# A second feed-forward product by seven products of quarters in place of eight, in network one

## Chip, core and metric

One core of one Trainium2 chip runs the whole program: two networks of two layers each, one after the other. Engines are named TensorE (PE), VectorE (DVE), ScalarE (ACT), GpSimd (POOL) and SyncE (SP). The metric is the device time of one execution in microseconds; the kernel before takes 3363.85 us (median of three).

## What is computed

Of the reference, the part that the change touches is the end of each layer of network one, at `SEQ` = 512 tokens, `D_MODEL` = 1024, `D_FF` = 4096, in float32:

```python
x = x + jnp.concatenate([o_a, o_b, o_c], axis=-1) @ w_out[l]
hf = rmsnorm(x, g_mlp[l])
x = x + jnp.square(jax.nn.relu(hf @ w_ff1[l])) @ w_ff2[l]
```

The second product, (512 x 4096) times (4096 x 1024), is what is computed in another way. Network two and the rest of network one stay as they are.

## The kernel before

Every float32 product is made of three products of `fp32r` halves (`product`, line 262): high by high, high by low, low by high. So each weight tile of 128 rows and 512 columns is split first: ScalarE rounds it to its high half (`make_hi`, line 233, or 235 where a gain is multiplied in) and VectorE subtracts that from the tile for the low half (`make_lo`, lines 245 and 248). Both halves go to `whl`, which holds two chunks of four tiles; chunk j may be split when TensorE is through with chunk j - 2 (`chunk_used`). The chunks come from HBM over SyncE into a ring of four slots of 1 MB (`load_up_to`); a slot is loaded again when its last chunk's low halves are made.

The stage is `out_and_feed_forward` (line 1754). After the output projection and the norm, the 4096 hidden features are taken in two halves of 2048. For each half:

- `ReluSquared`: the first product, for four feature tiles (128 features x 512 tokens) at a time, in four PSUM banks, over two weight chunks (eight depth tiles). ScalarE takes the relu of a bank (line 1729), VectorE multiplies it with the bank (line 1745) into `y`, ScalarE makes its high half (line 1710) and VectorE its low half (line 1714) in `u`.
- `ResidualAdd`: the second product, with `u` as the stationary operand and the weights moving, for two halves of 512 output columns, four chunks of weights each, four token tiles per chunk. VectorE adds each finished bank to `x` (line 685).

What each engine does, and in which order, is written out by hand in the methods `tensor`, `scalar`, `vector` and `gpsimd` of these classes. In this stage GpSimd only raises four values to a power (line 702). A second product of one half has 16 depth tiles x 4 token tiles x 2 column halves x 3 = 384 matmuls, so that 2048 features cost 384 and 1024 cost 192.

```python
(sh, sl), (mh, ml) = stationary, moving
nc.tensor.matmul(bank, sh, mh, start=start, stop=False)
nc.tensor.matmul(bank, sh, ml, start=False, stop=False)
return nc.tensor.matmul(bank, sl, mh, start=False, stop=stop)
```

The same classes of work also occur elsewhere and are read from there: line 1944 is a GpSimd product of 512 columns in network two, lines 876 to 883 are rotations on GpSimd in the first stage, and line 1897 is a VectorE step that reads PSUM.

Of the kernel before, what the change touches and what calls it, by code (L numbers as in the profile page):

```python
# [8 lines left out]
F32 = mybir.dt.float32  # L9
# [6 lines left out]
P = 128  # L16
# [65 lines left out]
def chunks_of(rows, cols, width=512, deep=4, row0=0, col0=0):  # L82
# [7 lines left out]
A_HALF, B_HALF = D_FF // 2, D_FF2 // 2  # L90
# [4 lines left out]
    ("w_ff1", chunks_of(DM, A_HALF)), ("w_ff2", chunks_of(A_HALF, DM)),  # L95
    ("w_ff1", chunks_of(DM, A_HALF, col0=A_HALF)), ("w_ff2", chunks_of(A_HALF, DM, row0=A_HALF // P)),
]
B_WEIGHTS = [
# [29 lines left out]
class Core:  # L128
# [38 lines left out]
    def start_layer(self, weights, drams, prefix, l):  # L167
        self.queue, self.offsets, at = [], [], {}
        for name, chunks in weights:
            for k, kt, n, w in chunks:  # L170
# [34 lines left out]
class SplitWeights:  # L205
# [52 lines left out]
    def wait_tile(self, pe, j, k):  # L258
        pe.wait_ge(self.lo_made, self.tiles[j] + k + 1)

# [1418 lines left out]
class ReluSquared:  # L1679

    def __init__(self, c, w, j0, i, F, hl, u, r, y, sems, free):
        self.c, self.w, self.j0, self.base, self.F, self.hl = c, w, j0, i * F, F, hl
        self.u, self.r, self.y, self.free, self.n_group = u, r, y, free, i * F // 4
        self.filled, self.relu_done, self.squared, self.his, self.los = sems

    def tensor(self, pe):
        w, c, hl = self.w, self.c, self.hl
        for g in range(self.F // 4):  # L1690
            for j in (self.j0 + 2 * g, self.j0 + 2 * g + 1):
                row, kt = w.plan[j][0:2]
                for b in range(4):
                    if row == 0:
                        self.free(pe, g, b)
                    for k in range(kt):
# [3 lines left out]
                        ins = product(c.nc, c.banks((4 * g + b) % 8), (w.part(j, 0, k)[:, s], w.part(j, 1, k)[:, s]),  # L1700
# [7 lines left out]
    def high(self, act, f):  # L1708
        act.wait_ge(self.squared, self.base + f + 1)
        self.c.nc.scalar.copy(self.u[:, 0, f, :], self.y[:, f % 4, :]).then_inc(self.his, 1)  # L1710

    def low(self, dve, f):
        dve.wait_ge(self.his, self.base + f + 1)
        self.c.nc.vector.tensor_tensor(self.u[:, 1, f, :], self.y[:, f % 4, :], self.u[:, 0, f, :].bitcast(F32),
                                       ALU.subtract).then_inc(self.los, 1)

    def scalar(self, act):
        for g in range(self.F // 4):
            j = self.j0 + 2 * g
            self.w.make_hi(act, j + 2)  # L1720
            for b in range(4):
                f = 4 * g + b
                if b == 3:
                    act.wait_ge(self.c.chunk_used, self.w.first + j + 2)
                else:
                    act.wait_ge(self.filled, 3 * (self.n_group + g) + b + 1)
                if self.base + f >= 4:
                    act.wait_ge(self.squared, self.base + f - 3)
                self.c.nc.scalar.activation(self.r[:, f % 4, :], self.c.banks(f % 8), ACT.Relu
                                            ).then_inc(self.relu_done, 1)  # L1730
                if f:
                    self.high(act, f - 1)
            self.w.make_hi(act, j + 3)
        self.high(act, self.F - 1)

    def vector(self, dve):
        for g in range(self.F // 4):
            j = self.j0 + 2 * g
            self.w.make_lo(dve, j + 2)
            for b in range(4):  # L1740
                f = 4 * g + b
                dve.wait_ge(self.relu_done, self.base + f + 1)
                if self.base + f >= 4:
                    dve.wait_ge(self.los, self.base + f - 3)
                self.c.nc.vector.tensor_tensor(self.y[:, f % 4, :], self.c.banks(f % 8), self.r[:, f % 4, :],
                                               ALU.mult).then_inc(self.squared, 1)
                if f >= 2:
                    self.low(dve, f - 2)
            self.w.make_lo(dve, j + 3)
        self.low(dve, self.F - 2)  # L1750
        self.low(dve, self.F - 1)


def out_and_feed_forward(c, mix, hl, gain, half, u, r, y):
# [3 lines left out]
    F = A_HALF // P  # L1758
    with ExitStack() as ctx:
        sb = lambda n, s: ctx.enter_context(nc.sbuf_tensor("aff_" + n, s, F32))  # L1760
        ssq, rstd, junk = sb("ssq", [P, TT, 2]), sb("rstd", [P, TT, 1]), sb("junk", [P, BANK])
        xn = y[:].rearrange("p f s -> p (f s)").rearrange("p (b n) -> p b n", b=2)
        with c.stage("aff", "hi", "lo", "mix_turned", "mix_his", "mix_los", "out_filled", "out_added", "squares",
                     "meaned", "rooted", "rows", "x_turned", "x_his", "x_los", "up_filled", "relu_done", "squared",
                     "u_his", "u_los", "down0_filled", "down0_added", "down1_filled", "down1_added", "end_squares") as (
                block, hi_made, lo_made, mix_turned, mix_his, mix_los, out_filled, out_added, squares,
                meaned, rooted, rows, x_turned, x_his, x_los, up_filled, relu_done, squared,
                u_his, u_los, down0_filled, down0_added, down1_filled, down1_added, end_squares):
            ups, downs = (4, 20), (12, 28)
            gains = {j: gain for j0 in ups for j in range(j0, j0 + 8)}  # L1770
            w = SplitWeights(c, ctx, "aff_", 36, hi_made, lo_made, gains)
# [8 lines left out]
                               (ssq, rstd, junk[:], xn, half))  # L1780

            def up_free(i):
                def free(pe, g, b):
                    if g >= 2:
                        pe.wait_ge(squared, i * F + 4 * (g - 1))
                    elif i == 0:
                        pe.wait_ge(x_los, 8)
                    else:
                        pe.wait_ge(down0_added, TT * (g + 1))
                return free  # L1790
            up = [ReluSquared(c, w, ups[i], i, F, hl, u, r, y, (up_filled, relu_done, squared, u_his, u_los),
                              up_free(i)) for i in range(2)]
            down = [ResidualAdd(c, w, pair(downs[i], 4), of(u), i * F, x, None,
                                ((down0_filled, down1_filled)[i], (down0_added, down1_added)[i]) + (None,) * 4,
                                lambda pe, n, t, i=i: pe.wait_ge(squared, i * F + F - 4 * (1 - n)),
                                lambda pe, n, t, k, i=i: pe.wait_ge(u_los, i * F + k + 1) if n == t == 0 else None)
                    for i in range(2)]
# [6 lines left out]
            def _(pe):  # L1804
# [3 lines left out]
                for i in range(2):  # L1808
                    up[i].tensor(pe)
                    down[i].tensor(pe)  # L1810
                pe.wait_ge(down1_added, 1)
                c.stay_busy(pe, 0, 40)

            @block.scalar
            def _(act):
# [5 lines left out]
                for i in range(2):  # L1821
                    up[i].scalar(act)
                    down[i].scalar(act)
                for t in range(TT):
                    act.wait_ge(down1_added, TT + t + 1)
# [5 lines left out]
            @block.gpsimd  # L1831
            def _(pool):
                out.gpsimd(pool)

            @block.vector
            def _(dve):
# [5 lines left out]
                for i in range(2):  # L1842
                    up[i].vector(dve)
                    down[i].vector(dve)
# [1660 lines left out]
def first_block(c, d, cst, layers=DEPTH):  # L3505
# [11 lines left out]
    with nc.Fori(0, layers) as l, ExitStack() as ctx:  # L3517
# [87 lines left out]
        with ExitStack() as right:  # L3605
            hl = split_tile(right)
            with nc.sbuf_tensor("a_shift", [P, 24], F32), \
                    nc.sbuf_tensor("a_u", [P, 2, A_HALF // P, SEQ], F32R) as u, \
# [268 lines left out]
```

## Time and profile before

| | |
|---|---|
| runs | 3363.85, 3378.34, 3363.09 us; median 3363.85 |
| profiled execution | span 3368.7 us from the first to the last instruction |
| granted TensorE clock, mean | 0.980 |
| TensorE busy | 3198.9 us, 95% |
| VectorE busy | 1884.3 us, 56% |
| ScalarE busy | 1311.1 us, 39% |
| GpSimd busy | 394.5 us, 12% |

The profiled execution's own time is told by its span alone; it lies 4.9 us above the median of the runs. Busy times of TensorE count each matmul from its start to its modelled end, so they overlap; the pace of matmuls is read from one start to the next. A line L245 is a line of the kernel before; where a helper issues an instruction the line is the helper's. The stage of the change lies at 308 to 721 us in layer 1 and at 1022 to 1435 us in layer 2.

### The profile page before, as it was taken

To read this page: it belongs to the slowest core of one execution; us is meant where nothing else is said; L and a number is where in the kernel's file an instruction comes from. 1 tells how busy PE (TensorE), PEld (TensorE's weight loads), DVE (VectorE), ACT (ScalarE), POOL (GpSimd) and SP (SyncE) were. 2 spreads that over 40 slices of the span, in tenths; PEclk is the share of its full clock that TensorE was granted. 3 is DMA by queue.
4 is the path that set the end of the run, shared out by engine and by line. 5 is a ranking of instruction groups with operands and counts; after the bars stand their busy time and mean duration, and the time that the engine had idled before them with its cause. 6 is when DMAs were issued, how large, how long until landed. Compare 5 with 4: busy or idle time off the path is not lost. (4 is left out here: it accounts for less than half of the span.)

```text
span 3368.7 us, 49442 instructions
## 1 busy us (share of the span) xinstructions
PE 3198.9 (95%) x19200; PEld 2657.4 (79%) x19200; DVE 1884.3 (56%) x3610; ACT 1311.1 (39%) x2780; POOL 394.5 (12%) x368
## 2 busy tenths in 40 slices
PE   8998999999989999979999999999899989999996
PEld 6877888877777888868867888888788768888885
DVE  4875443336865434247486457474475865574644
ACT  4455433334354424134363333233443543332324
POOL 1021000000030000003013302010012034010100
PEclk9999999999999999989899999999999999999998
DMA  4111222222102222132100122222222000222221
GB/s 166 54 51 38 88 100 88 88 77 86 66 1 76 100 97 91 38 123 94 51 1 2 40 71 100 97 99 85 81 97 74 1 1 5 91 94 102 91 99 42
DMA packets 37345, 239.58 MB, mean 71 GB/s; under 512 B 4464, under 2 KB 5232, under 8 KB 15088
## 3 DMA queue, kind: packets, MB, share of 16 engines
q1 hardware_dynamic: 36528, 234.21, 19.5%
q8 instruction: 158, 2.59, 0.3%
q10 hardware_dynamic: 576, 2.10, 0.2%
q14 instruction: 83, 0.68, 0.1%
HBM read 234.19 MB, written 2.10 MB: 70 GB/s over the span
## 5 line engine op out<-in xcount | busy, mean ns | idle before, releaser
L265 PE MATMUL ps<-b_hl,bff_whl 128*128 128x512 f32 x704 | 274.1, 389 | 3.1 <-DVE b_hl L630 3.1
L267 PE MATMUL ps<-b_hl,bff_whl 128*128 128x512 f32 x704 | 273.9, 389 | 0.0
L266 PE MATMUL ps<-b_hl,bff_whl 128*128 128x512 f32 x704 | 273.9, 389 | 0.0
L248 DVE SCALAR_TENSOR_TENSOR bff_whl<-ring,b_cols,bff_whl 128x512 fp32r<-128x512 f32 (+1 forms) x224 | 153.2, 745 | 197.3 <-ACT bff_whl L235 197.0
L245 DVE TENSOR_TENSOR aff_whl<-ring,aff_whl 128x512 fp32r<-128x512 f32 x160 | 99.8, 686 | 223.1 <-ACT aff_whl L233 223.1
L235 ACT ACTIVATE bff_whl<-ring,b_cols 128x512 fp32r<-128x512 f32 (+1 forms) x224 | 136.6, 682 | 176.4 <-PE ps L267 176.4
L266 PE MATMUL ps<-aff_whl,a_u 128*128 128x512 f32 x512 | 204.3, 399 | 0.0
L265 PE MATMUL ps<-a_hl,aff_whl 128*128 128x512 f32 x512 | 199.4, 390 | 3.1 <-DVE a_hl L630 3.1
L265 PE MATMUL ps<-aff_whl,a_u 128*128 128x512 f32 x512 | 201.7, 394 | 0.0
L267 PE MATMUL ps<-aff_whl,a_u 128*128 128x512 f32 x512 | 200.7, 392 | 0.0
L266 PE MATMUL ps<-a_hl,aff_whl 128*128 128x512 f32 x512 | 199.2, 389 | 0.0
L267 PE MATMUL ps<-a_hl,aff_whl 128*128 128x512 f32 x512 | 199.2, 389 | 0.0
L265 PE MATMUL ps<-ain_whl,a_hl 128*128 128x512 f32 (+3 forms) x512 | 189.3, 370 | 9.4 <-issue 6.2
L233 ACT CAST aff_whl<-ring 128x512 fp32r<-128x512 f32 x160 | 87.5, 621 | 275.9 <-PE ps L267 271.3
L266 PE MATMUL ps<-ain_whl,a_hl 128*128 128x512 f32 (+3 forms) x512 | 186.2, 364 | 0.0
L267 PE MATMUL ps<-ain_whl,a_hl 128*128 128x512 f32 (+3 forms) x512 | 186.0, 363 | 0.0
L245 DVE TENSOR_TENSOR bff_whl<-ring,bff_whl 128x512 fp32r<-128x512 f32 x128 | 84.6, 720 | 144.2 <-ACT bff_whl L233 144.2
L265 PEld LDWEIGHTS ps<-b_hl,bff_whl 128*128 128x128 f32 x704 | 132.1, 188 | 30.9 <-DVE b_hl L630 3.6
L248 DVE SCALAR_TENSOR_TENSOR aff_whl<-ring,a_gains,aff_whl 128x512 fp32r<-128x512 f32 x128 | 87.6, 746 | 122.3 <-ACT aff_whl L235 122.1
L267 PEld LDWEIGHTS ps<-b_hl,bff_whl 128*128 128x128 f32 x704 | 132.2, 188 | 27.6
L266 PEld LDWEIGHTS ps<-b_hl,bff_whl 128*128 128x128 f32 x704 | 132.2, 188 | 27.3
L233 ACT CAST bff_whl<-ring 128x512 fp32r<-128x512 f32 x128 | 70.4, 621 | 210.3 <-PE ps L267 202.8
(510 smaller groups left out, 7826.8 us busy)
## 6 DMA issues: line engine op xcount, KB each, us to landing
ring<-in_a_w_ff SPq DMA_DIRECT2D x64, 1024.0 KB, 4.6
ring<-in_b_w_up SPq DMA_DIRECT2D x32, 1024.0 KB, 4.8
ring<-in_a_w_in SPq DMA_DIRECT2D x16, 1024.0 KB, 4.9
ring<-in_b_w_down SPq DMA_DIRECT2D x16, 1024.0 KB, 4.6
ring<-in_b_w_in_att SPq DMA_DIRECT2D x12, 1024.0 KB, 4.6
ring<-in_b_w_up SPq DMA_DIRECT2D x16, 768.0 KB, 4.1
ring<-in_b_w_in_conv SPq DMA_DIRECT2D x12, 768.0 KB, 4.2
ring<-in_a_w_out SPq DMA_DIRECT2D x8, 1024.0 KB, 4.7
```

The costliest lines, as they stand in the source:

```text
L233: self.c.nc.scalar.copy(self.part(j, 0, k), src[:, k, :]).then_inc(self.hi_made, 1)
L235: self.c.nc.scalar.activation(self.part(j, 0, k), src[:, k, :], ACT.Copy, scale=g[:, row + k:row + k + 1]).then_inc(self.hi_made, 1)
L245: self.c.nc.vector.tensor_tensor(self.part(j, 1, k), src[:, k, :], self.part(j, 0, k).bitcast(F32), ALU.subtract).then_inc(self.lo_made, 1)
L248: self.c.nc.vector.scalar_tensor_tensor(out=self.part(j, 1, k), in0=src[:, k, :], scalar=g[:, row + k:row + k + 1], in1=self.part(j, 0, k) ...
L265: nc.tensor.matmul(bank, sh, mh, start=start, stop=False)
L266: nc.tensor.matmul(bank, sh, ml, start=False, stop=False)
L267: return nc.tensor.matmul(bank, sl, mh, start=False, stop=stop)
```

## The change

The hidden features are now taken in four pieces of 1024. A piece is its first product as before (`ReluSquared`, two groups of four feature tiles), then one second product (512 tokens x 1024 features) times (1024 features x 1024 columns) by Strassen's scheme in Winograd's form. The left side A has token halves and feature halves, the right side B feature halves and column halves of 512. With S1 = A21 + A22, S2 = S1 - A11, S3 = A11 - A21, S4 = A12 - S2 and T1 = B12 - B11, T2 = B22 - T1, T3 = B22 - B12, T4 = B21 - T2 the seven products are, in TensorE's order, M1 = A11 B11, M2 = A12 B21, M5 = S1 T1, M6 = S2 T2, M7 = S3 T3, M3 = S4 B22, M4 = A22 T4. Each has 2 token tiles, 4 depth tiles, 3 matmuls.

GpSimd makes the four sums S in `y` and `s12` (two groups of features per piece, 4 operations each) and the four combinations T (4 tiles each, T1 in `t1`, the others in place in the ring), and adds the common part `z` to the four quarters of `x` (8 operations): 32 operations of 512 columns per piece. M1 is copied to `z` by ScalarE; VectorE adds M6 and M7 to `z` and M2, M5 (twice), M3 and M4 to `x`. All seven left and seven right sides are split in halves. `u` becomes `u7` (named `a_u` in the program), seven sides by two halves.

```diff
+class MixedWeights(SplitWeights):
...
+    def combine(self, pool, block, which):
...
+        if which == SevenBlocks.T1:
+            self.c.wait_chunk(pool, block.ring)
+            self.c.wait_chunk(pool, block.ring + 2)
+            if i:
+                self.split_done(pool, self.blocks[i - 1], SevenBlocks.T1)
+            dst, x, y = t1, b[2], b[0]
+        elif which == SevenBlocks.T2:
+            self.c.wait_chunk(pool, block.ring + 3)
+            self.split_done(pool, block, SevenBlocks.B11)
...
+        for k in range(block.kt):
+            self.c.nc.gpsimd.tensor_tensor(dst[:, k, :], x[:, k, :], y[:, k, :], ALU.subtract
+                                           ).then_inc(self.combined, 1)
+
+    def slot_read(self, sp, i):
+        block, q = self.user[i - self.first]
+        if block is None:
+            sp.wait_ge(self.lo_made, self.tiles[q + 1])
+        elif q == 0:
+            self.split_done(sp, block, SevenBlocks.T2)
+            sp.wait_ge(self.combined, block.made_by(SevenBlocks.T4, block.kt - 1))
...
+class SevenSides:
...
+    def add(self, pool, group, size, rows):
...
+        tt(s1, a21, a22, ALU.add).then_inc(self.sums, 1)
+        pool.wait_ge(self.sums, n + 1)
+        tt(s2, s1, a11, ALU.subtract).then_inc(self.sums, 1)
+        pool.wait_ge(self.sums, n + 2)
+        tt(a21, a11, a21, ALU.subtract).then_inc(self.sums, 1)
+        pool.wait_ge(self.los, self.base(group) + self.A12 + 1)
+        tt(a12, a12, s2, ALU.subtract).then_inc(self.sums, 1)
...
+class SevenProducts:
...
+    def tensor(self, pe):
+        w, kt = self.w, self.block.kt
+        for m in range(7):
+            j = self.block.item + m
+            left = self.LEFT[m]
+            for a in range(2):
+                self.wait_bank(pe, m, a)
...
+                for group, size in self.groups:
+                    for _ in range(size // 2):
+                        if a == 0:
+                            w.wait_tile(pe, j, k)
+                            pe.wait_ge(self.sides.los, self.sides.base(group) + left + 1)
...
+class FeedForwardPiece:
...
+    def scalar(self, act):
...
+        w.make_hi(act, m + 2)
+        up.high(act, S.S2, 1)
+        down.keep(act, 0)
+        down.keep(act, 1)
+        w.make_hi(act, m + 3)
+        up.high(act, S.S3, 1)
+        w.make_hi(act, m + 4)
+        up.high(act, S.S4, 1)
+        up.high(act, S.A22, 1)
...
+    def gpsimd(self, pool):
+        w, up, down, block = self.w, self.up, self.down, self.block
+        M = SevenProducts
+        up.add(pool, 0)
+        w.combine(pool, block, SevenBlocks.T1)
+        w.combine(pool, block, SevenBlocks.T2)
+        up.add(pool, 1)
+        w.combine(pool, block, SevenBlocks.T3)
+        down.add_z(pool, M.UPPER_LEFT)
+        w.combine(pool, block, SevenBlocks.T4)
+        down.add_z(pool, M.UPPER_RIGHT)
+        down.add_z(pool, M.LOWER_LEFT)
+        down.add_z(pool, M.LOWER_RIGHT)
```

The order of two engines shows what stands where. On VectorE, from the last split that belongs to the first product's time on: before, in a second product of 2048 features (`aff_whl` is a split of weights, `a_u<-a_y` one of activations, `x<-ps` an addition from PSUM):

```order
L245 TENSOR_TENSOR aff_whl<-ring,aff_whl 128x512 x4
L1714 TENSOR_TENSOR a_u<-a_y,a_u 128x512 x2
L245 TENSOR_TENSOR aff_whl<-ring,aff_whl 128x512 x12
L685 TENSOR_TENSOR x<-ps,x 128x512 x4
L245 TENSOR_TENSOR aff_whl<-ring,aff_whl 128x512 x12
```

And now, in the second product of a piece, from the split of B21 to the additions of M5 (`a_s` is S1 or S2, `a_t` is T1):

```order
L360 TENSOR_TENSOR aff_whl<-ring,aff_whl 128x512 x4
L474 TENSOR_TENSOR a_u<-a_y,a_u 128x512
L474 TENSOR_TENSOR a_u<-a_s,a_u 128x512
L360 TENSOR_TENSOR aff_whl<-a_t,aff_whl 128x512 x4
L474 TENSOR_TENSOR a_u<-a_s,a_u 128x512
L360 TENSOR_TENSOR aff_whl<-ring,aff_whl 128x512 x4
L573 TENSOR_TENSOR x<-ps,x 128x512 x2
L474 TENSOR_TENSOR a_u<-a_y,a_u 128x512
L360 TENSOR_TENSOR aff_whl<-ring,aff_whl 128x512 x4
L573 TENSOR_TENSOR x<-ps,x 128x512
L576 TENSOR_TENSOR x<-ps,x 128x512
```

Splits of weights stood in long runs with four additions between them; now four splits, one or two low halves of the left side and two to four additions follow each other, one such set per product. On GpSimd the stage held this before:

```order
L702 TENSOR_TENSOR aff_rstd<-aff_rstd,const_a 128x1 x4
```

After it now stands, for each piece, a queue that begins with the first group's sums S and goes on so (L394 are T1, T2, T3 and T4, `a_t` is T1, L460 to L466 the second group's sums S, L588 adds `z`):

```order
L394 TENSOR_TENSOR a_t<-ring 128x512 x4
L394 TENSOR_TENSOR ring<-ring,a_t 128x512 x4
L460 TENSOR_TENSOR a_s<-a_y 128x512
L462 TENSOR_TENSOR a_s<-a_s,a_y 128x512
L464 TENSOR_TENSOR a_y<-a_y 128x2x256
L466 TENSOR_TENSOR a_y<-a_y,a_s 128x2x256
L394 TENSOR_TENSOR ring<-ring 128x512 x4
L588 TENSOR_TENSOR x<-x,a_r 128x512 x2
L394 TENSOR_TENSOR ring<-ring 128x512 x4
L588 TENSOR_TENSOR x<-x,a_r 128x512 x6
```

GpSimd's queue is in order: T1 stands behind the first group's sums, T3 behind the second group's, and T4 behind the first two additions of `z`.

## Rows read from the trace of the kernel before

**Rows 1.** Busy time and clock by stretch, layer 1; columns as in the first line
```profile
core 0: us, PE busy (x) PEld busy (x) DVE busy (x) ACT busy (x) POOL busy (x), PEclk, DMA share, GB/s
366.00:452.70 86.70, 86.70 (x384) 71.77 (x383) 38.67 (x60) 34.49 (x59) 0.00 (x0) 1.00 0.27 98
452.70:497.50 44.80, 44.80 (x193) 36.04 (x192) 14.37 (x23) 10.26 (x19) 0.00 (x0) 1.00 0.26 94
...
340.00:366.00 26.00, 22.94 (x126) 19.21 (x125) 14.60 (x26) 12.43 (x29) 2.22 (x4) 1.00 0.19 74
...
497.50:585.00 87.50, 87.50 (x382) 71.35 (x381) 31.83 (x49) 26.52 (x45) 0.00 (x0) 1.00 0.27 97
```

**Rows 2.** TensorE's waits, 366 to 640 us
```profile
engine line waited for: us in total, times, longest us
PE ps L265 <- DVE a_hl L630: 1.6, 1, 1.6
```

**Rows 3.** ScalarE's waits from 452.7 us; groups from 365 us (busy, mean ns)
```profile
ACT aff_whl L233 <- PE ps L267: 52.6, 6, 9.0
...
L233 ACT CAST aff_whl<-ring 128x512 fp32r<-128x512 f32 x32 | 17.5, 617 | 60.0 <-PE ps L267 60.0
L1745 DVE TENSOR_TENSOR a_y<-ps,a_r 128x512 f32<-128x512 f32 x24 | 16.5, 689 | 27.7 <-ACT a_r L1729 27.6
...
L1710 ACT CAST a_u<-a_y 128x512 fp32r<-128x512 f32 x23 | 14.1, 613 | 0.0
L685 DVE TENSOR_TENSOR x<-ps,x 128x512 f32<-128x512 f32 x8 | 5.5, 689 | 11.7 <-PE ps L267 11.7
```

**Rows 4.** Timeline, a chunk's split, nothing on GpSimd: start, duration, engine, line
```profile
498.44 2.50 DVE L245 TENSOR_TENSOR aff_whl<-ring,aff_whl 128x512 fp32r<-128x512 f32 x4
```

**Rows 5.** GpSimd operations of 512 columns: count, busy, mean ns
```profile
L2272 POOL TENSOR_TENSOR a_proj<-a_proj,const_a 128x512 f32<-128x512 f32 x4 | 5.1, 1265 | 0.0
```

**Rows 6.** Timeline: splits beside GpSimd at 36 us; without it at 2041 us
```profile
36.20 1.45 POOL L876 TENSOR_TENSOR a_q<-a_mix,const_a 128x576 f32<-128x576 f32 x1 [4.19 <-DVE a_mix L863]
36.44 7.28 DVE L248 SCALAR_TENSOR_TENSOR ain_whl<-ring,a_gains,ain_whl 128x512 fp32r<-128x512 f32 x4 [0.38 <-ACT ain_whl L235]
37.60 1.89 POOL L877 TENSOR_TENSOR a_q<-a_mix,const_a 128x576 f32<-128x576 f32 x1
39.56 1.76 POOL L879 TENSOR_TENSOR a_mix<-a_mix,const_a 128x576 f32<-128x576 f32 x1
41.28 1.88 POOL L880 TENSOR_TENSOR a_mix<-a_mix,const_a 128x576 f32<-128x576 f32 x1
...
2041.23 2.57 ACT L235 ACTIVATE bff_whl<-ring,b_cols 128x512 fp32r<-128x512 f32 x4 [5.50 <-PE ps L267]
2041.99 2.74 DVE L248 SCALAR_TENSOR_TENSOR bff_whl<-ring,b_cols,bff_whl 128x512 fp32r<-128x512 f32 x4 [5.33 <-ACT bff_whl L235]
```

**Rows 7.** VectorE's splits at line 245: ns min/median/max, first and last start
```profile
L245 DVE TENSOR_TENSOR bff_whl<-ring,bff_whl x128: 677/684/1793, 1914.1 to 3280.4; 128x512 fp32r<-128x512 f32 x128
```

**Rows 8.** VectorE reading PSUM, line 1897: same columns; and on the timeline
```profile
L1897 DVE SCALAR_TENSOR_TENSOR b_acc<-ps,b_cols,b_acc x176: 747/749/752, 1985.6 to 3218.8; 128x511 f32<-128x511 f32 x88, 128x510 f32<-128x510 f32 x88
...
2047.11 1.30 POOL L1944 TENSOR_TENSOR b_silus<-b_silus,b_acc 128x512 f32<-128x512 f32 x1 [81.36 <-DVE b_acc L1897]
2047.65 1.54 DVE L1897 SCALAR_TENSOR_TENSOR b_acc<-ps,b_cols,b_acc 128x511 f32<-128x511 f32 x2
```

**Rows 9.** Loads of the feed-forward weights: count, size, median us to landing
```profile
ring<-in_a_w_ff SPq DMA_DIRECT2D x64, 1024.0 KB, 4.6
```

**Rows 10.** Busy time and clock where the clock falls; columns as in rows 1
```profile
272.00:279.00 7.00, 4.22 (x33) 3.64 (x32) 0.72 (x3) 5.46 (x35) 0.46 (x2) 0.99 0.00 1
279.00:285.70 6.70, 4.53 (x14) 2.87 (x14) 3.39 (x8) 4.08 (x13) 5.59 (x4) 0.50 0.00 0
985.50:992.30 6.80, 4.34 (x39) 4.10 (x38) 0.00 (x0) 5.46 (x36) 0.68 (x3) 1.00 0.00 0
992.30:995.70 3.40, 2.90 (x6) 1.60 (x6) 1.61 (x5) 2.73 (x9) 0.82 (x2) 0.50 0.01 2
```

More of the change, by code:

```diff
@@ L86, in chunks_of, with quarters_of @@
             for n in range(0, cols, width) for k in range(0, tiles, deep)]
-A_HALF, B_HALF = D_FF // 2, D_FF2 // 2
+def quarters_of(k0, tiles, cols, width=512):
+    halves = [[(k0 + g + h * (min(4, tiles - g) // 2), min(4, tiles - g) // 2) for g in range(0, tiles, 4)]
+              for h in range(2)]
+    return [(k, kt, n, width) for n in range(0, cols, width) for rows in halves for k, kt in rows]
+JOINED = ("w_ff2",)
+B_HALF = D_FF2 // 2
+A_PIECE = 1024
+A_PIECES = D_FF // A_PIECE
 A_WEIGHTS = [
@@ L169, in start_layer @@
         for name, chunks in weights:
+            if name in JOINED:
+                chunks = [(a[0], a[1] + b[1], a[2], a[3]) for a, b in zip(chunks[0::2], chunks[1::2])]
             for k, kt, n, w in chunks:
@@ L1706, in tensor @@
                         ins.then_inc(self.filled, 1)
[L1708 to L1715, printed above, removed]
-    def scalar(self, act):
[L1718 to L1734, printed above, removed]
@@ L1736, in vector @@
-    def vector(self, dve):
[L1737 to L1751, printed above, removed]
@@ L1807, in _ @@
                 out.tensor(pe)
[L1808 to L1812, printed above, removed]
+                for piece in pieces:
+                    piece.tensor(pe)
+                pe.wait_ge(down_added, pieces[-1].down.added_by(SevenProducts.M6, 1))
+                c.stay_busy(pe, pieces[-1].down.banks[6], 40)
             @block.scalar
@@ L1820, in _ @@
                 out.scalar(act)
[L1821 to L1825, printed above, removed]
+                for piece in pieces:
+                    piece.scalar(act)
+                last = pieces[-1].down
+                for t, (m, a) in enumerate(((SevenProducts.M3, 0), (SevenProducts.M3, 1), (SevenProducts.M4, 0),
+                                            (SevenProducts.M4, 1))):
+                    act.wait_ge(down_added, last.added_by(m, a))
+                    if t == 2:
+                        act.wait_ge(z_added, 8 * A_PIECES)
                     if t:
@@ L1833, in _ @@
                 out.gpsimd(pool)
+                for piece in pieces:
+                    piece.gpsimd(pool)
             @block.vector
@@ L1841, in _ @@
                 out.vector(dve)
-                for i in range(2):
-                    up[i].vector(dve)
-                    down[i].vector(dve)
+                for piece in pieces:
+                    piece.vector(dve)
 class ConvGate:
```

384 lines of the change are left out of this document (352 added, 32 removed).

## The prediction

> **What bounds the kernel now.** I read the stage from 366 us on first. TensorE is busy for the whole of it at the full clock, in the first product and in the second [rows 1], and the only wait it shows there is one of 1.6 us [rows 2]. The second product's 192 matmuls take 44.80 us, 0.2333 us from one start to the next [rows 1]. ScalarE and VectorE wait for TensorE [rows 3]. So in this stage a matmul less is 0.2333 us less, as long as nothing new is late.
>
> Then the engines that get the new work. A VectorE subtraction that makes a low half takes 0.68 us; four in a row take 2.50 us, 0.60 us apart [rows 4]. A GpSimd operation of 512 columns takes 1.27 us [rows 5]. What matters is the two together. With GpSimd at work, four VectorE splits take 7.28 us (the same group without it: 2.57 us for ScalarE's, 2.74 us for VectorE's), and each GpSimd operation lasts 1.76 to 1.89 us where the first took 1.45 us: they take turns, one of each, though GpSimd's there are of 576 columns [rows 6]. With 512 columns the longest VectorE split is 1793 ns against the median of 684 ns: **1.10 us lost for each GpSimd operation met** [rows 7]. A VectorE operation with one input in PSUM loses nothing: L1897 runs under GpSimd, as at 2047.65 us, and all 176 last 747 to 752 ns [rows 8].
>
> **The sum on TensorE.** A piece has 7 products of 2 row tiles, 4 depth tiles and 3 matmuls: 168 where a quarter of the depth had 192. Four pieces in two layers: 8 x 24 = 192 matmuls less, 192 x 0.2333 = **44.8 us saved**. The first product has as many as before. The stationary operand still lies in `a_u`, moved within the same region, so I keep 0.2333 us; if it took the first product's 0.2267 us (366.00 to 452.70 us, about 383 matmuls [rows 1]), the 1344 that stay would give 1344 x 0.0066 = 8.9 us more. This is one end of the range, the other is nothing.
>
> **What is added, by engine, in a piece.** ScalarE: 12 splits of weights more (28 for 16) at 0.62 us [rows 3], 14 of activations for 8 at 0.61, two copies: 43 us of work in a piece of 82, on an engine that now waits 9.0 us at a time for TensorE [rows 3]; I cost it at nothing, and were it late, VectorE's splits would be late by as much. SyncE: a slot that GpSimd combines in place comes free later. The next piece's first chunk waits for T4 (30 us after the end of the first product, by the schedule below), lands 4.6 us later [rows 9] and is wanted at 40.5; the second is free at 39.8, lands at 44.4, wanted at 46.4. Two microseconds to spare: nothing, but thin. GpSimd: 32 operations of 512 columns, 40 us at 1.27. VectorE: 12 weight splits, 6 activation splits and 10 additions more.
>
> **Where it hurts: VectorE behind GpSimd.** Let 0 be the end of a piece's first product. VectorE starts afresh there, since its last square waits for that matmul and for ScalarE's relu (0.6 us). From then to the split of A22, whose lower rows the last product (M4) reads half-way through its first row tile, VectorE has 30 splits with both inputs in SBUF (B21, T1, T2, T3, B22, T4 at four each, and A12, S1, S2, S3, S4, A22) and 11 operations on PSUM (the square, 10 additions): 30 x 0.60 + 11 x 0.63 (a 0.69 us addition [rows 3], overlapped like the splits) = 24.9 us. TensorE's seven products last 7 x 24 x 0.2333 = 39.2 us, and A22 is wanted 4.2 us before their end, at 35.0. So VectorE has 35.0 - 0.6 - 24.9 = **9.5 us to lose**. In that stretch GpSimd has 18 operations (the last of T2, four sums S, four of T3, two additions, four of T4, three additions). If each met a split, VectorE would lose 18 x 1.10 = 19.8 us. I laid them side by side, each in its order, alternating when both want it:
>
> ```
> VectorE done, us: square 1.3, B21 7.7, A12 8.3, T1 15.7, S2 17.4, T2 19.8, S3 22.2, T3 29.0,
>                   M5's additions 31.5, B22 33.9, S4 36.3, T4 39.8, A22 42.2
> TensorE done, us: M1 5.6, M2 12.5, M5 19.2, M6 24.8, M7 32.5, M3 40.5, M4 46.4
> ```
>
> M2 waits 1.3 us for A12 (behind B21, which alternates with S1 to S3), M5 1.1 us for T1 (against T3's making), M7 2.1 us for T3 (against T4's), M3 2.4 us for S4, M4 0.3 us for A22. VectorE lost 42.2 - 0.6 - 24.9 = 16.7 us, 7.2 more than it had: **7.2 us of waits per piece, 8 x 7.2 = 57.6 us**. The queue behind S4 is T4's split and M7's additions; nobody but TensorE waits for those. ScalarE's part is never last in this schedule: it starts T3 when M5 is done, at 19.2, and VectorE comes to it at 23.4. In the first product the same contention (S1 to S4 and T1 on GpSimd against a split of four and six low halves) puts VectorE back to about -3.3 us, but it then waits for the last feature tile anyway: nothing. The two additions M3 and M4 and the squares behind the last piece lie as the old last additions did: nothing.
>
> **The sum:** -44.8 + 57.6 = +12.8 us. The profiled execution spans 3368.7 us, 4.9 above the median of the runs, 3363.85; carried to the median: **3377 us**, +0.4%. Break-even is at 44.8/8 = 5.6 us of waits per piece; a measurement of this kernel can tell about 0.5%, 17 us, from no change.
>
> [...]
>
> **Rivals.**
> 1. *The cover holds (faster).* If GpSimd's operations fall mostly on VectorE's PSUM operations and idle moments, so that VectorE loses at most 9.5 of the possible 19.8 us, TensorE never waits: -44.8, **3319 us**, and up to 3335 with 2 us per piece. For it: 9.5 us is half of what is possible, and before the change VectorE is busy only 31.83 of 87.50 us in the second product and the next first [rows 1]. Against it: GpSimd is released by the same squares and additions that release VectorE, and a group of four splits is long enough to meet three or four of its operations, as at 36.44 us [rows 6].
> 2. *The lock costs more (slower).* One mechanism: whole instructions one after the other, 1.95 us a pair, 1.35 lost in place of 1.10. Its place is the same stretch; 16.7 x 1.35/1.10 = 20.5 us lost, 11.0 too many per piece, 88 us in all: +43, **3407 us**. It decides once a meeting costs more than 1.0 us (15.1 us lost per piece is break-even). For it: each dependent pair of GpSimd operations also passes a semaphore, and VectorE's additions wait for several. Against: rows 6 and 7 have the shorter turn.
> 3. *The clock falls (slower).* The granted clock fell to 0.50 for 6.7 and 3.4 us after stretches in which TensorE was busy 4.22 of 7.00 and 4.34 of 6.80 us [rows 10]; it stayed at 1.00 with 22.94 of 26.00 [rows 1]. M3 with its wait is busy 5.6 of 8.0 us, between these. A fall of 6.7 us in each piece would cost half of it, 8 x 3.4 = 27 us: **3404 us**. For it: 70% is nearer to the first pair. Against: what ran there were 128-column and narrower products, here 512-column ones. The Trainium skill (TensorE: Matmul & The Clock Gate, "What's actually happening") lets the clock fall only after an idle window; TensorE is never idle for long in this forecast, so by that rule this rival does not come. The trace does not agree in full: the clock fell with TensorE busy 60% of the time [rows 10].
> 4. *It does not do what it says.* Excluded for the count: the order of the program has 672 matmuls on `a_u` in a layer against 768.
>
> **How the numbers follow.** Forecast, with waits of 4 to 10 us per piece: 48% (own range 3351 to 3399). Rival 1: 27%, for my hand schedule is the weakest part and half a dozen meetings less decide. Rival 2: 14%. Rival 3: 11%. Faster by over 0.5% (below 3347): all of rival 1 and 0.06 of the forecast (its low end with the 8.9 us of the faster pitch), 0.33. Within 0.5%: 0.27 of the forecast and 0.02 of rival 3, 0.29. Slower: 0.15 + 0.14 + 0.09 = 0.38. The range holds 8 in 10 and takes in rivals 2 and 3 and all but the last few microseconds of rival 1: **3322 to 3414 us**. Since both signs hold much, the forecast's own range is the one given above.
>
> **What would show it.** Right: splits of 1.7 to 1.8 us on VectorE beside GpSimd, some 14 to 16 of them per piece; TensorE waiting in M2, M5, M7 and M3 for VectorE's splits, about 58 us in all in this stage; the first product still 0.2267 us a matmul and unbroken; additions on `ps` at 0.69 us; clock 1.00. Wrong: a piece's second product in under 41 us (rival 1) or over 49 us (rival 2); a clock of 0.50 in the stage (rival 3); TensorE waiting for ScalarE, for GpSimd or for a chunk of the ring instead; waits inside the first product.

## The result and the profile after

The kernel after takes 3395.68 us (median of four runs, 3392.07 to 3403.57), against 3368.02 us (3363.09 to 3378.34) for the kernel before on the same chip: ratio 1.008, 95% interval 1.0056 to 1.0103. So it is slower, by 28 us. The forecast was 3377 us, with a range of 3322 to 3414 us.

The page of the profiled execution (its own time 3392.65 us), first the busy time of each engine, then groups, then an issue of DMA:

```profile
span 3390.8 us, 49996 instructions
PE 3181.9 (94%) x19008; PEld 2636.0 (78%) x19008; DVE 2241.4 (66%) x3834; ACT 1400.4 (41%) x2940; POOL 804.8 (24%) x624
L360 DVE TENSOR_TENSOR aff_whl<-ring,aff_whl 128x512 fp32r<-128x512 f32 x224 | 227.0, 1071 | 30.2 <-ACT aff_whl L348 30.2
L594 PE MATMUL ps<-aff_whl,a_u 128*128 128x512 f32 x448 | 190.5, 425 | 43.1 <-DVE a_u L474 33.2
L348 ACT CAST aff_whl<-ring 128x512 fp32r<-128x512 f32 x224 | 122.3, 620 | 167.2 <-PE ps L596 162.5
ring<-in_a_w_ff SPq DMA_DIRECT2D x64, 1024.0 KB, 4.8
```

TensorE has 192 matmuls less and 17 us less of busy time, VectorE 357 us more. Line 360 is the old line 245, the split of a weight tile: its mean is 1071 ns where a free one takes 0.68 us. Line 594 is the first of the three matmuls that the helper `product` issues (448 times on `a_u`); it waits 33.2 us in all for line 474, the split of a left side. Before, TensorE had one wait of 1.6 us between 366 and 640 us [rows 2].

The stretches of the stage, columns as in [rows 1]: the first product of layer 1's second piece, its second product, the next first product, a first and a second product of layer 2, and two moments in that last one:

```profile
455.30:498.80 43.50, 43.50 (x193) 36.02 (x192) 32.46 (x37) 18.45 (x31) 16.37 (x12) 1.00 0.34 118
498.80:547.50 48.70, 43.34 (x169) 33.53 (x168) 47.17 (x46) 20.34 (x37) 35.28 (x22) 0.93 0.20 74
547.50:591.10 43.60, 43.60 (x194) 36.06 (x193) 31.45 (x36) 18.44 (x31) 16.33 (x11) 1.00 0.31 111
1189.90:1233.50 43.60, 43.60 (x194) 36.06 (x193) 31.44 (x36) 18.45 (x31) 16.32 (x11) 1.00 0.31 108
1233.50:1282.10 48.60, 43.23 (x170) 33.47 (x168) 47.11 (x46) 20.34 (x37) 35.20 (x22) 0.93 0.20 76
1243.30:1246.70 3.40, 3.40 (x9) 2.63 (x8) 3.40 (x3) 0.00 (x0) 3.40 (x3) 0.50 0.00 0
1270.60:1274.00 3.40, 3.27 (x8) 2.63 (x9) 3.40 (x5) 0.00 (x0) 1.12 (x1) 0.50 0.00 0
```

A first product is as before, 43.5 to 43.6 us, unbroken. A second product of 168 matmuls takes 48.6 us (47.5 in the very first), where 192 took 44.8 [rows 1] and 168 without a wait would take 39.2. VectorE is busy for 47 of the 48.6 us. And the granted clock falls to 0.50 twice, 3.4 us each time, which no row of before shows in this stage. From the first matmul of the first piece to the last of the last piece, layer 1 goes from 353.5 to 367.9 us and layer 2 from 353.5 to 368.8 us: **+29.7 us**. The span grew by 22.1 us, since the rest of the program was 7.6 us shorter in this execution than in the one profiled before.

What TensorE waits for in that second product (us in all, times, longest):

```profile
PE ps L594 <- DVE a_u L474: 4.1, 2, 2.2
PE ps L594 <- DVE aff_whl L360: 1.2, 2, 0.7
```

All of it is VectorE. ScalarE, GpSimd and the ring of chunks are in none of the waits from 360 to 735 us.

The lines of VectorE over the whole run (ns min/median/max, first and last start):

```profile
L360 DVE TENSOR_TENSOR aff_whl<-ring,aff_whl x224: 674/680/1790, 308.0 to 1457.7; 128x512 fp32r<-128x512 f32 x112
L360 DVE TENSOR_TENSOR aff_whl<-a_t,aff_whl x32: 1755/1768/1784, 417.2 to 1432.3; 128x512 fp32r<-128x512 f32 x32
L573 DVE TENSOR_TENSOR x<-ps,x x64: 671/675/692, 428.1 to 1466.6; 128x512 f32<-128x512 f32 x64
```

This is [rows 7] again with more of it. T1, whose four tiles lie in `a_t`, is split at 1.77 us every single time; the additions that read PSUM take 0.68 us with GpSimd at work beside them. The start of a second product, with 0 at 1233.5 us (start, duration; four in a row are told as one):

```profile
1234.30 0.69 DVE L2057 TENSOR_TENSOR a_y<-ps,a_r 128x512 f32<-128x512 f32 x1 [0.56 <-ACT a_r L2048]
...
1234.91 6.88 DVE L360 TENSOR_TENSOR aff_whl<-ring,aff_whl 128x512 fp32r<-128x512 f32 x4
...
1236.12 1.74 POOL L460 TENSOR_TENSOR a_s<-a_y 128x512 f32<-128x512 f32 x1
...
1237.93 1.62 POOL L462 TENSOR_TENSOR a_s<-a_s,a_y 128x512 f32<-128x512 f32 x1
...
1239.63 1.61 POOL L464 TENSOR_TENSOR a_y<-a_y 128x512 f32<-128x512 f32 x1
...
1241.72 0.68 DVE L474 TENSOR_TENSOR a_u<-a_y,a_u 128x512 fp32r<-128x512 f32 x1
...
1242.54 0.48 PE L594 MATMUL ps<-aff_whl,a_u 128*128 128x512 f32 x1 [1.91 <-DVE a_u L474]
...
1243.34 0.63 PE L594 MATMUL ps<-aff_whl,a_u 128*128 128x512 f32 x1
```

The four splits of B21 take 6.88 us; meanwhile GpSimd ends the last operation of T2 and makes S1, S2 and S3, one operation for each split. Only then does the split of A12 start, 0.68 us by itself, and M2, which had reached its third depth tile, has idled 1.91 us for it. 0.8 us after it starts again its matmuls last 0.63 us in place of 0.40: the clock has fallen.

### The profile page after: what moved, and what is told of

The parts are those of the page before. It is cut to its first block and busy times, and to the rows that moved or that the text cites. A ratio compares the mean times of both kernels' runs of the same rounds, so it can differ in the third digit from the quotient of the medians.

```text
span 3390.8 us, 49996 instructions
## 1 busy us (share of the span) xinstructions
PE 3181.9 (94%) x19008; PEld 2636.0 (78%) x19008; DVE 2241.4 (66%) x3834; ACT 1400.4 (41%) x2940; POOL 804.8 (24%) x624
## 5 line engine op out<-in xcount | busy, mean ns | idle before, releaser
L360 DVE TENSOR_TENSOR aff_whl<-ring,aff_whl 128x512 fp32r<-128x512 f32 x224 | 227.0, 1071 | 30.2 <-ACT aff_whl L348 30.2
L594 PE MATMUL ps<-aff_whl,a_u 128*128 128x512 f32 x448 | 190.5, 425 | 43.1 <-DVE a_u L474 33.2
L2371 POOL TENSOR_TENSOR b_silus<-b_silus,b_acc 128x512 f32<-128x512 f32 x44 | 70.7, 1606 | 550.0 <-DVE b_acc L2324 550.0
L348 ACT CAST aff_whl<-ring 128x512 fp32r<-128x512 f32 x224 | 122.3, 620 | 167.2 <-PE ps L596 162.5
L595 PE MATMUL ps<-aff_whl,a_u 128*128 128x512 f32 x448 | 186.4, 416 | 0.0
L596 PE MATMUL ps<-aff_whl,a_u 128*128 128x512 f32 x448 | 184.6, 412 | 0.0
L363 DVE SCALAR_TENSOR_TENSOR aff_whl<-ring,a_gains,aff_whl 128x512 fp32r<-128x512 f32 x128 | 126.1, 1044 | 74.6 <-ACT aff_whl L350 74.6
L594 PEld LDWEIGHTS ps<-b_hl,bff_whl 128*128 128x128 f32 x704 | 132.1, 188 | 31.1 <-DVE b_hl L959 3.6
L596 PEld LDWEIGHTS ps<-b_hl,bff_whl 128*128 128x128 f32 x704 | 132.1, 188 | 27.4
```

Of the source, the lines that this page charges most:

```text
L348: self.c.nc.scalar.copy(self.part(j, 0, k), src[:, k, :]).then_inc(self.hi_made, 1)
L360: self.c.nc.vector.tensor_tensor(self.part(j, 1, k), src[:, k, :], self.part(j, 0, k).bitcast(F32), ALU.subtract).then_inc(self.lo_made, 1)
L363: self.c.nc.vector.scalar_tensor_tensor(out=self.part(j, 1, k), in0=src[:, k, :], scalar=g[:, row + k:row + k + 1], in1=self.part(j, 0, k) ...
L2371: self.c.nc.gpsimd.tensor_tensor(self.silus[:, m, :], self.silus[:, m, :], self.acc[:, (self.all + f) % 4, :], ALU.mult).then_inc(self.tim ...
```

## The experiments

The theory: each GpSimd operation that reads SBUF and meets a two-input VectorE operation costs VectorE 1.1 us; with some 17 of them between a piece's first product and its last, VectorE is behind TensorE by more than seven products give back. Rivals: the clock is what costs; or TensorE's waits come from the order in which work stands on VectorE (or on TensorE itself) and not from the amount.

**GpSimd nearly without work.** All its 32 operations of a piece stay, with all waits, but of 4 columns per block or 8: what is left out is nearly all columns of S, T and the additions of `z`. The sums S, not shown below, are narrowed in the same way, and `s12` and `t1` are filled once ahead of the stage.

```diff
-            self.c.nc.gpsimd.tensor_tensor(dst[:, k, :], x[:, k, :], y[:, k, :], ALU.subtract
+            self.c.nc.gpsimd.tensor_tensor(dst[:, k, 0:8], x[:, k, 0:8], y[:, k, 0:8], ALU.subtract
...
-            self.c.nc.gpsimd.tensor_tensor(dst, dst, self.z[:, a, :], ALU.add).then_inc(self.z_added, 1)
+            self.c.nc.gpsimd.tensor_tensor(dst[:, 0:8], dst[:, 0:8], self.z[:, a, 0:8], ALU.add).then_inc(self.z_added, 1)
```

> Left out: nearly all columns of GpSimd's sums S, combinations T and additions of z; every GpSimd instruction, every wait and every other engine's work stays, but each is 8 columns wide. Theory (VectorE's splits lose 1.10 us to each wide GpSimd operation they meet): no split over 0.8 us, VectorE reaches A22 by about 26 us after the first product, TensorE has no wait, a piece's second product takes 168 x 0.2333 = 39.2 us, clock 1.00 in the stage; about 45 us faster than the kernel before (0.987). Rival (VectorE's own added work and order make it late, GpSimd or not): second product stays at 45 us or more and the kernel no faster than before.

3326.84 us, ratio 0.985 (0.9825 to 0.9875). A second product, and line 360:

```profile
493.40:532.60 39.20, 39.20 (x169) 31.55 (x168) 29.74 (x48) 20.24 (x37) 6.08 (x20) 1.00 0.25 90
```

```profile
L360 DVE TENSOR_TENSOR aff_whl<-ring,aff_whl x224: 681/685/694, 309.4 to 1385.6; 128x512 fp32r<-128x512 f32 x112
```

39.2 us in all eight pieces, the clock at 1.00, no split above 694 ns. TensorE's own part of the change is worth what the prediction took for it: 8 x (44.8 - 39.2) = 44.8 us, at 0.2333 us a matmul and not at 0.2267.

**GpSimd writes and doesn't read.** Narrow operations are also short ones, so that this leaves open whether it is GpSimd's reading that holds VectorE up or its being busy at all. Here each of the 32 is a fill of the same 512 columns, so that all of GpSimd's arithmetic is left out; the edits of S and `z`, not shown, are of the same kind.

```diff
-            self.c.nc.gpsimd.tensor_tensor(dst[:, k, :], x[:, k, :], y[:, k, :], ALU.subtract
-                                           ).then_inc(self.combined, 1)
+            self.c.nc.gpsimd.memset(dst[:, k, :], 0.5).then_inc(self.combined, 1)
...
```

> Left out: all of GpSimd's arithmetic in the stage; each of its 32 operations per piece is a memset of the same 512 columns, which writes SBUF and reads nothing (about half a microsecond each). If it is the reading that locks VectorE out, no split is over 0.8 us, the second product takes 39.2 us and the ratio is 0.985 to 0.988 as with narrow operations. If any wide GpSimd operation locks VectorE out, splits of 1.0 to 1.3 us appear beside memsets.

3327.64 us, ratio 0.9852 (0.9836 to 0.9869); all eight second products take 39.2 us. GpSimd's group of T, and line 360:

```profile
L394 POOL MEMSET ring<- 128x512 f32 x48 | 23.1, 525 | 28.6 <-DVE aff_whl L360 28.6
```

```profile
L360 DVE TENSOR_TENSOR aff_whl<-ring,aff_whl x224: 680/687/695, 314.8 to 1385.6; 128x512 fp32r<-128x512 f32 x112
```

GpSimd works 0.525 us at a time beside the same splits and not one of them lasts over 695 ns. So it is neither that GpSimd is at work nor that it writes; of what these two runs changed, the reading is left. (An operation that reads one input was not tried.) The Trainium skill (SBUF — State Buffer, "Who interferes with whom") says the same: two SBUF inputs on VectorE contend with a GpSimd instruction that reads SBUF, "not with one that only writes it"; the trace agrees.

**Only the combinations T narrow.** The first edit above alone: S and the additions of `z` stay whole, half of GpSimd's work.

> Left out: nearly all columns of the combinations T (16 of the 32 wide GpSimd operations of a piece); sums S and additions of z stay wide. Theory of the lock: in the stretch that decides, 9 of 18 meetings go, VectorE loses about 8 us instead of 17, under the 9.5 it has, but the sums still meet B21's split, so A12 is late by up to 1 us: second product 39.2 to 41 us, 30 to 45 us faster than before (0.988 to 0.991). Rival (the additions of z and the sums, which wait for others, are what delays): second product over 44 us.

3331.54 us, ratio 0.9874 (0.9851 to 0.9897). A second product, and TensorE's wait in the four of layer 1:

```profile
497.50:537.70 40.20, 39.38 (x169) 31.45 (x168) 37.32 (x44) 20.26 (x37) 23.88 (x20) 1.00 0.23 82
```

```profile
PE ps L594 <- DVE a_u L474: 3.3, 4, 0.8
```

Of 9.4 us of waits 1.0 is left, the one for A12 behind S1 to S3. 122 splits are still over 1 us, against 221 in the kernel after, and yet 8.4 of 9.4 us are gone. In the trace VectorE is through with A22 at 35.4 us after the first product, so it has lost 35.4 - 0.6 - 24.9 = 9.9 us. That fits a slack of about 9.5 us, as the prediction had it: meetings inside it cost nothing but the one late start in M2.

**The clock by itself.** The full computation, with 9 matmuls more in M2 and 10 in M3, into a bank that is not in use, placed where TensorE would idle; VectorE has the same work.

```diff
+                        u = self.sides.u7
+                        if a == 0 and k == 2 and m in (self.M2, self.M3):
+                            spare = self.M5 if m == self.M2 else self.M4
+                            self.wait_bank(pe, spare, 0)
+                            for _ in range(9 if m == self.M2 else 10):
+                                self.c.nc.tensor.matmul(self.bank(spare, 0), u[:, left, 0, 0, s], w.part(j, 0, 0),
+                                                        start=True, stop=True)
...
```

> The full computation, and in M2 and M3, ahead of the third depth tile, 9 and 10 extra matmuls of 512 columns into a bank that is free (2.1 and 2.3 us), so that TensorE works where it would wait for A12 and S4. If the falls of the clock to 0.50 for 3.4 us that follow these two waits cost what they seem to (about 1.3 us of a second product of 48.6), they go, a second product takes 46.5 to 47.5 us, and the kernel is 8 to 15 us faster than the changed one (1.004 to 1.006 of before). Rival (the clock costs nothing, since TensorE would wait for VectorE anyway): second product stays at 48.6 us or longer, ratio 1.008 to 1.010.

3395.46 us, ratio 1.0064 (1.0046 to 1.0083).

```profile
1230.60:1278.30 47.70, 45.27 (x189) 34.52 (x188) 47.16 (x45) 20.34 (x37) 35.24 (x22) 1.00 0.19 67
```

The clock stays at 1.00 and a second product ends 1.0 us sooner (47.6 to 47.7 for 48.6 us), a little less than expected. So the falls cost 1.0 us a piece, 8 in all, not the bulk. The whole time cannot show 8 us (1.0064 against 1.008, and the intervals overlap); this rests on the trace. The kernel after holds the same comparison: its very first second product is the only one with a single fall (the one in M2 and none in M3), and it takes 47.5 us:

```profile
407.80:455.30 47.50, 41.93 (x170) 32.22 (x169) 46.93 (x45) 20.33 (x37) 35.05 (x22) 0.96 0.19 70
```

So here the fall in M3 is the one that is paid; the one in M2 is taken up by the wait for T1 that M5 would otherwise have. The next run shows that wait.

**VectorE's order.** Splits that TensorE waits for go ahead of additions that nobody waits for.

```diff
         w.make_lo(dve, m + 4)
+        up.low(dve, S.S4, 1)
+        up.low(dve, S.A22, 1)
+        w.make_lo(dve, m + 5)
+        w.make_lo(dve, m + 6)
         down.add(dve, M.M5, 0)
         down.add(dve, M.M5, 1)
-        w.make_lo(dve, m + 5)
         down.add(dve, M.M6, 0)
         down.add(dve, M.M6, 1)
-        up.low(dve, S.S4, 1)
-        w.make_lo(dve, m + 6)
+        w.make_lo(dve, m + 7)
         down.add(dve, M.M7, 0)
         down.add(dve, M.M7, 1)
-        up.low(dve, S.A22, 1)
-        w.make_lo(dve, m + 7)
```

> The full computation; only VectorE's order in the second product is changed: the low halves of S4 and A22 and the splits of B22 and T4 come ahead of the additions of M5 and M6, and the next chunk's split ahead of M7's. Theory: the same meetings with GpSimd, but the additions, which nobody waits for, take the late places. M3 no longer waits for S4 nor M4 for A22, the clock falls once per piece instead of twice; waits in M2, M5 and M7 stay. Second product 43.5 to 45.5 us, 25 to 40 us faster than the changed kernel, about level with the one before (0.996 to 1.001). Rival (what counts is the total that VectorE has to do by the end of a piece): second product stays near 48 us.

3373.96 us, ratio 1.0003 (0.9988 to 1.0017).

```profile
1224.10:1268.80 44.70, 41.51 (x170) 32.47 (x169) 44.16 (x44) 20.33 (x37) 28.89 (x18) 0.96 0.21 79
```

3.9 us a piece come back. M3 and M4 no longer wait. The clock falls once, in M2, in six of the eight pieces; in the last piece of each layer it does not, behind the same wait of 1.9 us for A12:

```profile
680.30:725.00 44.70, 40.54 (x169) 31.02 (x168) 42.68 (x45) 18.43 (x34) 30.57 (x20) 1.00 0.00 1
```

There M2 takes 7.8 us and not 9.3, but M5 then takes 1.1 us more, waiting for T1, and M7 0.5 us more, and the second product takes the same 44.7 us: the fall in M2 is free, and a wait of that length does not bring one every time. 44.7 us for 168 matmuls is what 192 took before, so the kernel is as fast as before: the gain and the contention cancel.

**TensorE's order.** In a product the two row tiles are now inside the loop over depth tiles, so that the third depth tile of a left side, whose split is late in M2 and M3, is wanted after 12 matmuls and not after 6.

```diff
-            for a in range(2):
-                self.wait_bank(pe, m, a)
-                s = slice(a * P, (a + 1) * P)
-                k = 0
-                for group, size in self.groups:
-                    for _ in range(size // 2):
+            k = 0
+            for group, size in self.groups:
+                for _ in range(size // 2):
+                    for a in range(2):
+                        if k == 0:
+                            self.wait_bank(pe, m, a)
+                        s = slice(a * P, (a + 1) * P)
...
```

> The full computation; only TensorE's loops inside a product are exchanged: depth tile outside, row tile inside, so it asks for a new depth tile every 1.4 us in place of 0.7, while a contended split delivers one every 1.70 us. Theory: same VectorE schedule to 0.3 us; the waits for A12 (M2), T1 (M5), T3 (M7) and S4 (M3) each shrink by up to 1.4 us, and with shorter waits the clock falls less. Second product 44 to 46 us in place of 48.6, ratio to before 0.998 to 1.003. Rival (TensorE follows VectorE's total): 48 us or more.

3391.31 us, ratio 1.0047 (1.0034 to 1.006). A second product, and its waits:

```profile
1224.20:1270.40 46.20, 41.74 (x169) 30.69 (x168) 45.65 (x44) 20.33 (x37) 33.75 (x22) 1.00 0.16 58
```

```profile
PE ps L596 <- DVE a_u L474: 2.1, 3, 1.3
PE ps L596 <- DVE x L578: 1.4, 1, 1.4
```

Less than expected: 2.4 us a piece, not 2.6 to 4.6, and the ratio is above the 0.998 to 1.003 too. The clock no longer falls, and the waits are shorter, but both banks of a product now end together and M4 waits 1.4 us until VectorE has read one.

**Both orders.**

> The full computation with both: VectorE's order of e4_dve_order and the exchanged loops. Theory: M3 and M4 have no wait, M2, M5 and M7 a short one, no fall of the clock in the stage: second product 41 to 43.5 us, ratio to before 0.991 to 0.996, the first full computation that is faster than before. Rival (waits only move): 44.7 us as with VectorE's order alone, ratio 1.000.

3368.78 us, ratio 0.9992 (0.9979 to 1.0005).

```profile
1210.00:1254.40 44.40, 41.57 (x169) 30.78 (x169) 43.83 (x44) 20.34 (x37) 28.92 (x18) 1.00 0.21 80
```

A miss: 44.4 us, where 41 to 43.5 were expected, and 0.3 us less than with VectorE's order alone. VectorE is busy 43.8 of the 44.4 us, which points to its total as what sets the end now. The next change takes some of that total away.

**And GpSimd's order.** T1 stands ahead of the first group's sums, T3 ahead of the second group's, so that more of GpSimd's work falls into the first product, where VectorE has time.

```diff
-        up.add(pool, 0)
         w.combine(pool, block, SevenBlocks.T1)
+        up.add(pool, 0)
         w.combine(pool, block, SevenBlocks.T2)
-        up.add(pool, 1)
         w.combine(pool, block, SevenBlocks.T3)
+        up.add(pool, 1)
```

> The full computation: the one before it, and GpSimd makes T1 ahead of the first group's sums and T3 ahead of the second group's. Theory: two or three of its 18 operations leave the stretch that decides for the time in which VectorE waits for TensorE: second product 0.5 to 2.5 us shorter than without, ratio 0.987 to 0.994. Rival: T3 ahead delays S1 to S3, which M5 and M6 need, and nothing is gained (within 0.5 us of the one before it, or longer).

**3349.73 us, ratio 0.9926 (0.9914 to 0.9938)**: the full computation, faster than both kernels (0.7%, clear of the interval). A second product; and the timeline around its longest product, M2:

```profile
1195.50:1237.10 41.60, 40.17 (x169) 31.24 (x168) 40.76 (x43) 20.24 (x37) 24.94 (x16) 1.00 0.22 85
```

```profile
1196.27 4.71 POOL L394 TENSOR_TENSOR ring<-ring 128x512 f32<-128x512 f32 x3
...
1196.95 6.28 DVE L360 TENSOR_TENSOR aff_whl<-ring,aff_whl 128x512 fp32r<-128x512 f32 x4
...
1203.15 1.78 DVE L474 TENSOR_TENSOR a_u<-a_y,a_u 128x512 fp32r<-128x512 f32 x1
...
1205.07 0.47 PE L596 MATMUL ps<-aff_whl,a_u 128*128 128x512 f32 x1 [1.01 <-DVE a_u L474]
```

GpSimd is busy 24.9 us in the stretch instead of 28.9, VectorE 40.8 instead of 43.8, the product 2.8 us shorter (0.5 to 2.5 were expected). 170 splits are over 1 us, 51 fewer than in the kernel after. What is left is A12, still behind B21, now with T3's making in place of S1 to S3 between the splits.

**GpSimd's order alone**, in the kernel after:

> The full computation: the changed kernel with GpSimd's order alone altered (T1 ahead of the first group's sums, T3 ahead of the second group's). Lock theory: about two and a half operations fewer in the deciding stretch, VectorE 2 to 3 us sooner at S4 and A22: second product 45.5 to 47 us in place of 48.6, ratio to before 1.001 to 1.005. Rival (GpSimd's order matters only with VectorE's): 48 us or more. If it is under 45 us, moving T3 spares more meetings than the count says.

3391.8 us, ratio 1.006 (1.0041 to 1.0079). Four second products take 46.0 to 46.1 us and four 47.0 to 47.4, about as expected; the ratio is just above what was. Two of them, the second of layer 2 and the third of layer 1:

```profile
1226.60:1272.50 45.90, 41.38 (x169) 32.41 (x168) 43.55 (x44) 20.23 (x37) 31.16 (x20) 0.96 0.19 70
589.20:636.60 47.40, 42.81 (x170) 33.71 (x169) 44.05 (x46) 20.23 (x37) 31.64 (x20) 0.93 0.22 80
```

What parts the two kinds is the clock: in each of the four shorter ones it falls once, in each of the four longer ones twice, in M2 and in M3. That is the cost of the second fall again, 1.0 to 1.4 us. In all this order brings 1.2 to 2.6 us a piece alone, and 2.8 behind the other two.

**A12 ahead of B21.** In the version with all three orders, ScalarE and VectorE make the last depth tiles of A12 before B21's splits.

```diff
             up.square(dve, g, 3)
+            if g == 1:
+                up.low(dve, S.A12, g)
             w.make_lo(dve, j + 2 * g + 3)
-            up.low(dve, S.A12, g)
+            if g == 0:
+                up.low(dve, S.A12, g)
...
```

> The full computation: the version with VectorE's, TensorE's and GpSimd's orders changed, and in the second group A12's halves are made ahead of B21's splits on ScalarE and VectorE. There M2 is the one product still long (7.3 us for 5.6), and the lock theory says it waits for A12 behind four contended splits of B21. With A12 first, B21's tiles come 1.70 us apart from about 4 us and M2 asks for them 1.4 us apart from 5.6: M2 takes 5.6 to 6.2 us, a second product 40.0 to 41.0, and the kernel is 5 to 13 us faster than without (ratio to before 0.988 to 0.992). Rival (VectorE's total in the stretch still sets the end, so M5 or M7 wait instead): second product stays at 41.6 us.

3350.49 us, ratio 0.9937 (0.9919 to 0.9955), no different from 0.9926.

```profile
1210.90:1252.70 41.80, 40.91 (x169) 30.97 (x168) 40.31 (x43) 20.36 (x37) 24.53 (x16) 1.00 0.22 83
```

A miss: 40 to 41 us and 0.988 to 0.992 were expected. The wait only moved. A12 is there in time, but M2 still takes 7.4 us here (up to 8.3 in the first piece), since B21's splits, 1.70 us apart, now pace it: four of them need 6.8 us, a product 5.6.

## Why the prediction was right and wrong

**The matmuls saved.** 192 fewer at 0.2333 us: right. GpSimd idle gives back 44.8 us, and the faster pitch that was kept as an end of the range did not come.

**The price of a meeting.** 0.60 us for a split and 1.10 for the meeting make 1.70 us, and the splits beside GpSimd start 1.70 us apart. A split lasts at most 1790 ns; 14 per piece, up to A22, take 1.76 to 1.79 us, where 14 to 16 were forecast, and three more 1.37 to 1.48 us. Rival 2, whole instructions of 1.27 and 0.68 us one after the other, 1.95 us a pair, fails. Operations with an input in PSUM lose nothing: right (0.68 us).

**What was costed at nothing.** ScalarE, SyncE's chunks, the last additions and the first product: right, TensorE waits for none of them, the chunks land 4.8 us after issue, and the first product is unbroken.

**The schedule by hand** was the working most doubted and held: against the trace, counted from 1233.5 us,

| VectorE done with, us | B21 | A12 | T1 | S2 | T2 | S3 | T3 | M5 adds | B22 | S4 | T4 | A22 |
|---|---|---|---|---|---|---|---|---|---|---|---|---|
| forecast | 7.7 | 8.3 | 15.7 | 17.4 | 19.8 | 22.2 | 29.0 | 31.5 | 33.9 | 36.3 | 39.8 | 42.2 |
| measured | 8.3 | 8.9 | 16.3 | 18.0 | 20.4 | 23.0 | 29.8 | 32.2 | 34.6 | 37.1 | 40.6 | 43.1 |

0.6 us is there from B21 on and 0.9 at the end, so VectorE lost 17.6 and not 16.7 us. Most of the 0.6 us is B21's own: its four splits took 6.88 us, where the schedule gave them 6.4, for each of the four meets an operation.

**The step that failed is the size of the term "7.2 us of waits per piece": it measured 9.4** (48.6 less 39.2; 9.4 x 8 = 75 us, less 44.8 is +30, which is the stage's 29.7). The sum therefore said +12.8. Its parts: 0.9 us is VectorE's lateness above. From A22's split at 43.1 us the last product needs 4.2 us, which gives 47.3; the piece with no fall in M3 takes 47.5, and the version with filler 47.6, so 0.2 to 0.3 us are left over, perhaps handovers. The other 1.0 us is the clock: in M3, behind the wait for S4, its matmuls run at 0.50 for 3.4 us, M3 ends at 43.0 to 43.1 us and not at 41.5 as in the piece without that fall, and M4 then starts too late to wait for A22. The place of the waits was right for M2 (2.1 us measured for 1.3), M7 (1.8 for 2.1) and M3 (2.4 for 2.4); the two falls add 1.6 us each to M2 and M3, and 2.1 + 1.8 + 2.4 + 3.2 are the 9.4 us but for rounding. The forecast wait of 1.1 us in M5 did not appear, because the slow clock in M2 used it up: with VectorE's order changed it is there, 1.1 us, in the two pieces where the clock did not fall. The waits in M2, M7 and M3 came out within 0.8 us of what had been worked out; the clock, forecast at 1.00 for this stage, is the largest part of what the term left out.

**Rival 3** was thus not a case of its own but a part of the forecast: the clock falls in every piece, for 3.4 us twice and not 6.7 once, and costs 1.0 us and not 3.4, since more than half of what it takes lies in front of a wait. Against it the prediction held that 512-column matmuls run here and 128-column and narrower ones in [rows 10] (whose first stretch also holds four of 256 and 384 columns); the clock fell all the same. The Trainium skill (TensorE: Matmul & The Clock Gate, "What's actually happening") asks for an idle window before a fall. By that rule a second product would take the 47.6 us of the version with filler; the trace has 48.6 and does not agree, for TensorE had idled only 1.91 and 2.21 us when its clock fell.

**Rival 1**, the cover, fails, though by little: VectorE had 9.5 us to lose and lost 17.6. By 1.10 us each, seven or eight meetings fewer in each piece would have done; the version with three orders changed has 170 long splits for 221, six fewer a piece.

The time lies in the range and on the side that had the largest chance, 0.38. Of the 18.7 us between 3377 and 3395.68, 4.2 are the median of the kernel before, which four runs put at 3368.02 and not 3363.85; 8 x 2.2 = 17.6 are the term above; and what is left over, 3 us, goes the other way.

## What to carry to other kernels

What follows is shown for this kernel alone. Before work is put on GpSimd beside VectorE, count the meetings of its SBUF-reading operations with VectorE operations that have two inputs in SBUF, at 1.1 us each for 512 float32 columns, against the slack of VectorE in that stretch; here a saving of 5.6 us a piece on TensorE bought 17.6 us of meetings on VectorE. If it is over the slack by a little, order the three queues so that splits go ahead of additions that nobody waits for, depth tiles are wanted as late as can be, and GpSimd's work lies where VectorE waits anyway: together that made +0.8% into -0.7%, where each alone did not get below zero. And behind each new wait of TensorE read the granted clock: a fall made the product behind it 1.6 us longer here, of which between nothing and 1.4 us reached the end of the piece.

## What the hardware showed

- The granted clock fell to 0.50 (1.2 GHz) for 3.4 us behind a single TensorE wait of 1.91 or 2.21 us, with 512-column matmuls at full pace ahead of it. It stayed at 1.00 with TensorE's order alone changed, where the longest wait was 1.4 us. The length of the wait does not settle it: with VectorE's order alone changed, all eight pieces had the same wait of 1.9 us in M2 and six of them a fall.
- VectorE and GpSimd took turns, one operation each, where both had work waiting: T1's 32 splits all took 1755 to 1784 ns and started 1.70 us apart.
- A GpSimd fill of 512 columns takes 525 ns, an operation with two inputs 1.27 to 1.30 us by itself and 1.74 us beside VectorE's splits; the first costs VectorE's splits nothing (687 ns median), the second 1.1 us each.
- A clock fall can be free: that in M2 ended in front of another wait. With VectorE's order changed, pieces with it and without it both took 44.7 us.
